# Gathered value rows of the last 64 tokens: the first rows land in the running sums, a fourth place lies over the residual, and a round's two sums stand in two tiles

## What is computed

```python
def peer(h, wq, sub_keys, u_tab, v_tab):
    ...
        qq = (hx @ wq).reshape(pb, PEER_HEADS, 2, PEER_HALF)
        s = jnp.einsum('nhcd,hckd->nhck', qq, sub_keys).astype(jnp.float32)
        s1, i1 = lax.top_k(s[:, :, 0], PEER_TOPK)
        s2, i2 = lax.top_k(s[:, :, 1], PEER_TOPK)
        ...
        top, sel = lax.top_k(cand, PEER_TOPK)
        eidx = jnp.take_along_axis(cidx, sel, axis=-1)
        g = jax.nn.softmax(top, axis=-1)
        a = jax.nn.gelu(jnp.einsum('nd,nhkd->nhk', hx, u_tab[eidx]).astype(jnp.float32), approximate=False)
        w = (g * a).astype(hx.dtype)
        return jnp.einsum('nhk,nhkd->nd', w, v_tab[eidx])
    ...
    x = x + (ga * y_conv + gb * y_nsa) @ P['w_o']
    x = x + peer(rmsnorm(x, P['norm_ffn']), P['peer_wq'], P['peer_sub_keys'], P['peer_u'], P['peer_v'])
```

## Time and profile before

| | |
|---|---|
| median of three runs | 1196.44 us (1188.22 to 1201.93) |
| the profiled execution: its time | 1196.77 us |
| its span, first to last instruction | 1195.1 us |
| PE busy | 96% of the span |
| DVE busy | 75% |
| POOL busy | 52% |
| ACT busy | 51% |
| HBM read, written | 246.18 MB, 20.09 MB |
| v stage, first tile's start to the span's end | 829.37 to 1195.1 us |

### The profile page before, as it was taken

The page is one execution under the profiler, slowest core; times in us unless marked ns, Lnnn a source line. Parts: engine busy times, 40 slices in busy tenths (PEclk is TensorE's granted clock), DMA queues, the critical chain, the costliest instruction groups (busy, mean ns, idle before and its releaser), DMA issues.

```text
span 1195.1 us, 22982 instructions
## 1 busy us (share of the span) xinstructions
PE 1147.2 (96%) x8076; PEld 1087.6 (91%) x8076; DVE 897.1 (75%) x1599; ACT 604.5 (51%) x1159; POOL 624.2 (52%) x515
## 2 busy tenths in 40 slices
PE   7999999999999999999999999999979999988998
PEld 6698989978899999999999999999878998877998
DVE  6478456654686799999957887886776887876985
ACT  5355455432353454554556777755434554443552
POOL 2422234431000287877688777031787888887820
PEclk9999899899999999999999999999999999999999
DMA  6773439767765267677675666688888998888973
GB/s 245 271 228 88 142 104 344 231 191 258 211 235 174 98 180 174 167 171 187 171 184 144 162 168 162 195 262 287 313 297 270 318 321 287 290 290 283 326 274 124
DMA packets 129251, 263.64 MB, mean 221 GB/s; under 512 B 34608, under 2 KB 68976, under 8 KB 128432
## 3 DMA queue, kind: packets, MB, share of 16 engines
q1 hardware_dynamic: 89568, 208.08, 52.6%
q0 software_dynamic: 36848, 50.69, 17.2%
q10 hardware_dynamic: 2720, 3.40, 0.8%
HBM read 246.18 MB, written 20.09 MB: 223 GB/s over the span
## 4 chain that ended last, share of the span: by engine, by line
PE 73%; POOL 9%; issue 7%; DVE 5%; DMA 3%; ACT 2%; POOLq 1%; another core or an unknown queue 0%; ACTq 0%; DVEq 0%
PE ps L2297 26%; PE ps L2302 13%; PE ps L2372 9%; PE ps L2379 5%; POOL arena L677 5%; POOL arena L686 2%; PE ps L1843 2%; PE ps L2007 2%; PE ps L2110 2%; PE ps L1863 2%; DMA arena<-in_v,aux 2%; POOL aux L677 1%; PE ps L2148 1%; PE ps L2346 1%; PE ps L2115 1%
## 5 line engine op out<-in xcount | busy, mean ns | idle before, releaser
L1046 ACT ACTIVATE w_hi<-ring 128x1024 fp32r<-128x1024 f32 x280 | 296.8, 1060 | 366.3 <-issue 171.8
L1543 DVE TENSOR_TENSOR w_lo<-ring,w_hi 128x1024 fp32r<-128x1024 f32 x271 | 330.0, 1222 | 117.3 <-ACT w_hi L1046 83.2
L2297 PE MATMUL ps<-h_hi,w_hi 128*128 128x288 f32 x1088 | 294.9, 299 | 0.5 <-ACT w_hi L1046 0.5
L666 POOL DMA_INDIRECT gates<-arena x128 | 241.6, 1887 | 68.8 <-issue 44.9
L2297 PE MATMUL ps<-h_lo,w_hi 128*128 128x288 f32 x1024 | 277.3, 295 | 0.0
L2297 PEld LDWEIGHTS ps<-h_hi,w_hi 128*128 128x128 f32 x1088 | 205.5, 189 | 1.2 <-ACT w_hi L1046 1.0
L677 POOL DMA_INDIRECT arena<-in_v,aux x110 | 149.2, 1357 | 88.4 <-PE ps L2346 49.1
L2297 PEld LDWEIGHTS ps<-h_lo,w_hi 128*128 128x128 f32 x1024 | 192.8, 188 | 0.0
L2302 PE MATMUL ps<-h_hi,w_lo 128*128 128x288 f32 x1088 | 168.1, 297 | 2.1 <-DVE w_lo L1543 2.1
L2372 PE MATMUL ps<-h_hi,w_hi 128*128 128x448 f32 x672 | 154.5, 373 | 4.9 <-issue 3.0
L2302 PEld LDWEIGHTS ps<-h_hi,w_lo 128*128 128x128 f32 x1088 | 152.3, 189 | 2.6 <-DVE w_lo L1543 2.6
(11 more groups left out here) (377 smaller groups left out, 1968.1 us busy)
## 6 DMA issues: line engine op xcount, KB each, us to landing
ring<-in_uT SPq DMA_DIRECT2D x128, 512.0 KB
ring<-in_v SPq DMA_DIRECT2D x128, 512.0 KB
ring<-in_wout SPq DMA_DIRECT2D x32, 512.0 KB
ring<-in_wT SPq DMA_DIRECT2D x28, 512.0 KB
gates<-aux SPq DMA_DIRECT2D x32, 256.0 KB, 5.9
ring<-in_wtok SPq DMA_DIRECT2D x8, 512.0 KB
act_kept<-arena SPq DMA_DIRECT2D x32, 128.0 KB
aux<-gates SPq DMA_DIRECT2D x16, 256.0 KB
```

What stands on the lines that cost most here:

```text
L666: pool.indirect_dma_start(gates, bass.IndirectOffsetOnAxis(rt("gi")[:, P + s:P + s + 1].bitcast(U32), 0), rt("gi")[:, s:s + 1], None, comp ...
L1046: act.activation(w_hi[e % 2][:, :], ring[:, (W_O + e) % RING, :], ACT.Copy).then_inc(S["w_high"], 1)
L1543: dve.tensor_tensor(w_lo[e % 2][:, :], ring[:, (W_O + e) % RING, :], w_hi[e % 2][:, :].bitcast(F32), ALU.subtract)\
L2297: last = pe.matmul(ps[:, bank, 0:NT], w_hi[e % 2][:, k * P:(k + 1) * P], mov[:, k, :], start=(k == 0 and mov is mov_hi), stop=False, skip_ ...
```

## The change

1. **Places.** Slot 0's rows go straight into the two running sums (`IN_SUMS`), and DVE multiplies them there in place. Slots 1 and 2 take places 0 and 1. A fourth place, `OVER_X`, is the first 2048 columns of `xT`; slots 3, 6, 10, 14 and so on to 26 lie there. The place over the gates serves slots 7, 11, ... From slot 27 on, three places are left.
2. **POOL's order.** Twelve row transfers instead of eight are issued before the wait for the activations (slots 1, 2, then slot 0, whose x = 0 part also waits for `qq_or_sums`, the last use of that memory in the u stage). The wait for PE's tile (`row_tile(i)`) is gone; what remains is `rows_used` of the slot before in the place, once `lo_used` for the end of the u stage, once `weighed`, and `s_weights` before the values.
3. **Tiles of the sums.** x = 0 stands in a slot's tile and x = 1 in the next. Slots 0 to 3 are at tiles 8, 11, 14, 17; slots 4 to 26 at 20 to 104, one every 27/7 = 3.857 tiles; slots 27 to 31 at 107, 110, 113, 116 and 119 (x = 1 at 120).
4. **The residual.** Since `xT` is a place until slot 26, SP reads it back at tile 115 (`X1_AT`) and not at tile 8. The constant stays at tile 8.

```diff
+OVER_X, OVER_GATES, IN_SUMS = HELD, HELD + 1, HELD + 2
+LAST_OVER_X = 26
+def slot_place(i):
+    if i == 0:
+        return IN_SUMS
+    if i < FOUR:
+        return i - 1
+    return i % FOUR if i <= LAST_OVER_X else (OVER_GATES, 0, 1)[(i - LAST_OVER_X - 1) % 3]
 def slot_tile(i):
-    return row_tile(i + 1) + 2 if i < WIDER - HELD else row_tile(i + 2) + 1
-def slot_place(i):
-    return i % HELD if i < WIDER else (i - WIDER + HELD) % (HELD + 1)
+    if i < FOUR:
+        return 8 + 3 * i
+    return 20 + (i - FOUR) * 27 // 7 if i <= LAST_OVER_X else slot_tile(LAST_OVER_X) + 3 * (i - LAST_OVER_X)
...
-SLOT_AT = {slot_tile(i): i for i in range(SLOTS)}
-SUM_AT = PK - 6
+SLOT_AT = {slot_tile(i) + x: (i, x) for i in range(SLOTS) for x in range(2)}
+SUM_AT, X1_AT = PK - 6, PK - 13
...
                 if t == 2 * RING:
                     sp.wait_ge(S["lo_used"], E_V)
+                    sp.dma_start(e_ident, A["consts"][:, CONST["ident"][0]:CONST["ident"][1]]).then_inc(S["x1_back"], 16)
+                if t == X1_AT:
+                    sp.wait_ge(S["rows_used"], 2 * LAST_OVER_X + 2)
                     sp.dma_start(xT[:, :, :], x1_kept).then_inc(S["x1_back"], 16)
-                    sp.dma_start(e_ident, A["consts"][:, CONST["ident"][0]:CONST["ident"][1]]).then_inc(S["x1_back"], 16)
...
-            for i in range(HELD):
+            for i in (1, 2):
                 for x in range(2):
                     gather_rows(x, i)
+            gather_rows(1, 0)
+            pool.wait_ge(S["qq_or_sums"], Q_TILES + GROUPS)
+            gather_rows(0, 0)
             for i in range(2):
                 pool.wait_ge(S[f"act_out{i}"], 16 * PK // STAGE // 2)
             for k in range(4 * FOUR):
                 gather_value(k)
-            for i in range(HELD, SLOTS):
-                pool.wait_ge(S["lo_used"], E_V + row_tile(i))
-                if i == WIDER:
+            pool.wait_ge(S["lo_used"], E_V)
+            for i in range(3, SLOTS):
+                if i == FOUR + OVER_GATES:
                     pool.wait_ge(S["weighed"], PIECES_IN)
                 for x in range(2):
                     if earlier_slot(i) >= 0:
                         pool.wait_ge(S["rows_used"], 2 * earlier_slot(i) + x + 1)
                     gather_rows(x, i)
...
-            def weigh_slot(i):
+            def weigh_slot(i, x):
-                if i % FOUR == 0:
+                if i % FOUR == 0 and x == 0:
...
-                for x in range(2):
-                    w = e_weights[:, NS * x + i:NS * x + i + 1]
+                w = e_weights[:, NS * x + i:NS * x + i + 1]
...
                 if t in (SUM_AT + 1, SUM_AT + 3):
                     dh = (t - SUM_AT) // 2
                     dve.wait_ge(S["so_turned"], 2 + dh + 1)
+                    dve.wait_ge(S["x1_back"], 32)
...
                 if t == HALF:
-                    dve.wait_ge(S["x1_back"], 32)
+                    dve.wait_ge(S["x1_back"], 16)
```

More of the change, by code:

```diff
@@ L703, in _ @@
                     gather_rows(x, i)
-                if i % FOUR == HELD:
-                    pool.wait_ge(S["s_weights"], 2 + i // FOUR + 1)
-                for k in range(2 * (i + 2 * FOUR - HELD), 2 * (i + 2 * FOUR - HELD) + 2):
+                for k in range(4 * FOUR + 2 * (i - 3), 4 * FOUR + 2 * (i - 3) + 2):
                     if k < 2 * SLOTS:
+                        b = k // (2 * FOUR)
+                        if k % (2 * FOUR) == 0:
+                            pool.wait_ge(S["s_weights"], 2 + b - 2 + 1)
                         gather_value(k)
@@ L1806, in weigh_slot @@
                 dve.wait_ge(S["s_weights"], 2 + i // FOUR + 1)
[L1807 to L1815 removed]
+                w = e_weights[:, NS * x + i:NS * x + i + 1]
+                dve.wait_ge(S[row_sems[x][slot_place(i)]], row_base[x][slot_place(i)] + 32 * place_uses(i))
+                if i == 0:
+                    last = dve.tensor_scalar(e_sums[x], e_rows[x][IN_SUMS], w, None, ALU.mult)
+                else:
+                    dve.wait_ge(S["rows_used"], 2 * (i - 1) + x + 1)
+                    last = dve.scalar_tensor_tensor(out=e_sums[x], in0=e_rows[x][slot_place(i)], scalar=w, in1=e_sums[x], op0=ALU.mult, op1=ALU.add)
+                last.then_inc(S["rows_used"], 1)
             mov_low_part(1)
```

23 lines of the change are left out of this document (7 added, 16 removed).

## The result

| | before | after |
|---|---|---|
| median | 1196.87 us (1184.06 to 1210.69, 20 runs) | 1188.13 us (1178.22 to 1205.67, 20 runs) |
| profiled execution, span | 1195.1 us | 1181.0 us (its time 1182.7) |
| tile 0 to tile 122 of the v stage | 829.37 to 1171.77 | 828.14 to 1157.72 |

The ratio is 0.994, 95% interval 0.991 to 0.997: 7 us faster by the ratio, 9 by the medians, where 26 us were forecast. The time lies outside the range (1161 to 1186).

What follows compares the result with a forecast made beforehand. POOL's issuing of transfers was taken to bound the v stage, losing 36 us. Tile 122's end at 1146.2 plus a 20.8 us tail gave 1167.0, the residual's 2 us 1169 of span, forecast as 1171 us, range 1161 to 1186.

Steps and rivals of the forecast that it cites:

- What bounds the kernel: v stage: 36 us of PE time are lost, because POOL's issuing of transfers makes rows late, not the number of places.
- Part 1: POOL in the v stage: starts slot 3 at 855.8 us, issues 164 transfers, values' slots at 1.67 us each, ends at 1136.3.
- Part 2: Rows against DVE's sums: next to nothing lost up to slot 26; in the last five slots POOL is slower than wanted.
- Part 3: End of the v stage: last rows land at 1140.3, tile 122 ends at 1146.2, plus 20.8 us gives a span of 1167.0.
- the floor: The span with no loss in the v stage: 123 tiles of 2.51 us and the unchanged tail, 1158.9 us.
- rival 2: v stage: ring loads become the bound and ACT's three long idles (10.7 us) add to the sum; 1182 us, chance 0.13.
- Rival 1: v stage: POOL keeps up with DVE's less dense work and nearly nothing is lost; 1161 us, chance 0.14.
- Rival 4: v stage: DVE is late for another reason, such as its own 86% load; within 12 us of before, chance 0.06.
- Rival 3: v stage: without a pace POOL's issues grow to 2.0 us each, deciding from 1.88; 1216 us, chance 0.07.
- The pace is gone: POOL's start in the v stage: no 2.54 us hold by PE's tile, so slot 3 starts at 855.8 us.
- Part 4: Remaining edits: moving the residual's read costs 2 us (0 to 4.3); two tiles for sums and the fourth place count nothing.
- The rule against the trace: DVE and POOL exclude each other at SBUF, so POOL would run faster beside less dense DVE work, making the sum too high.

Runs made afterwards that it cites:

- b_noval: The kernel before the change without the 48 value gathers that follow the first 16; 1164.94 us, ratio 0.970.
- a_tiny: The changed kernel with row gathers of slots 1 to 31 bringing 16 of 512 columns, as many transfers; 1193.56 us, ratio 0.988.
- a_halfring: The changed kernel with SP loading only half of every v tile, columns 0 to 511 of 1024; 1188.39 us, ratio 0.990.
- a_paced: The changed kernel with a pace put back: POOL waits before a slot's rows until PE is within nine tiles of the slot's tile; 1178.74 us, ratio 0.985.
- a_paced_2: a_paced run again on another chip; 1175.37 us, ratio 0.984.
- a_one: The changed kernel with both sums of a slot put back into one tile; 1192.08 us, ratio 0.991.
- a_nogates: The changed kernel without the 17 gate loads that SP puts between the loads of v tiles 0 to 16; 1183.86 us, ratio 0.987.
- third chip: Ran the changed kernel with POOL zero writes replacing 48 value gathers (1161.94 us), with three waits a slot (1163.86), and with whole-row gathers plus pace (1160.98).

## Why the prediction was wrong

**What bounds the kernel: right.** 36 us were lost, and the number of POOL's transfers made the rows late: b_noval has no row wait and 0.970 of the time. But rows were not all of it: about 13 of the 36 us stood in tiles that waited for a late signal of PE (8 and 9, 25 to 27, 93 to 95; an estimate from the tiles' lengths less 2.51 us).

**Part 1, POOL's work: right to a microsecond.** Timeline of POOL after: the first row gather of slot 3, and the last two of slot 31.

```profile
856.18 0.95 POOL L684 DMA_INDIRECT xT<-in_v,aux  x1 [0.30 <-issue]
...
1133.26 1.83 POOL L684 DMA_INDIRECT arena<-in_v,aux  x1 [0.30 <-issue]
1135.39 0.95 POOL L684 DMA_INDIRECT arena<-in_v,aux  x1 [0.30 <-issue]
```

Forecast were a start at 855.8, `xT` as the target and an end at 1136.3; it was 1135.39 + 0.95 = 1136.34. But it contains 20 us of waits for places, so POOL was faster than 1.67 us a transfer, (280.2 - 20.4) / 164 = 1.58. Two errors met, so the match is luck.

**Part 2, rows in time: right.** 0.2 us of idle before the sums.

**Part 3, the sum: this step failed.** It took "tile 122 ends when the last rows have been added" and let the floor cover all that isn't rows. Tile 122 started at 1157.72, not at 1143.7, and not because of any row: the last sums stood early and PE was late all the same, which the prediction had named as the sign of a wrong mechanism. The term that failed is the loss beside rows: 0 beyond the residual's 2 us in the sum, 23 us in the trace, where `w_hi` and `w_lo` wait for signals that PE gives up to 7.6 us late. The 8 us that the sum left for rows were not lost, so two errors partly cancel. It could be seen before: ACT's idles of 4.30, 3.62 and 2.81 us with an unseen releaser, which the prediction read as late ring loads and priced in rival 2 at 10.7 us and a chance of 0.13. Each of the three ends 0.07 us after an update of `hi_used` (852.32, 911.67, 1100.26), for halves that PE had ended 3.6 to 5.7 us earlier.

**Rival 2, ring loads, was nearest in time (1182) and wrong in cause.** Its own test, ACT's waits for the ring over 15 us, came out at 5.0. a_tiny and a_halfring take the bytes away, and the time stays.

**The other rivals.** Rival 1 asked for under 1.6 us a transfer; POOL had 1.58, and the time was still lost elsewhere. Rival 4 (the losses stay, for another reason) holds the measured time within its 12 us, at a chance of 0.06, but it named DVE's own load. In mechanism it is the nearest, since it alone has DVE late for a reason other than rows or loads. Rival 3's rate of 1.88 us was never near.

**"The pace is gone" was priced as a gain; it was a loss.** a_paced and a_paced_2 stand at 0.985 and 0.984, the changed kernel at 0.994, so dropping the pace costs 10 to 12 us. The rest of the change is worth 18 to 19 us, where 26 were forecast. The prediction took the pace for a mere delay (5.9 us in 6 waits). With it, signals are late less often (27 and 26 starts for 43).

**Part 4.** *Residual's read*: forecast 2 us, measured none; from 1130.19 us, when SP issues it, to tile 122 every tile takes 2.51 or 2.52 us. Moving it away from tile 8 didn't win the 2.6 us carried over from there either: that cluster was no work of the residual's, and grew from 3 to 10 us. *Two tiles for the sums*: nothing, as forecast (a_one). *Fourth place*: "a place isn't what POOL waits for" is wrong for the changed kernel, where POOL waits 20 us for places; what those waits are worth isn't shown, since a fourth place was not tried alone. *Gate loads*: at most a few us (a_nogates).

**The rule against the trace.** The Trainium skill, "SBUF — State Buffer", section "SBUF: two separate sides", has DVE and GpSimd take turns at a shared port. For POOL the trace agrees in direction: its issue takes 0.95 us where DVE rests and often 1.4 to 2.0 beside it. It is tempting to read the late `w_lo` as the other half of the rule, POOL holding DVE up. The trace doesn't bear that out: each of them starts 0.09 us after PE's signal. The same section says that ACT's port waits on no one, and ACT's idles of 3 to 15 us are no evidence against it, since ACT too was waiting for PE's signals.

**What stays open.** Why PE's updates come late beside POOL's indirect issues is not known; that they do, and that they come within 2.2 to 2.4 us of a burst's end, is. Nor is it known why a cluster begins where it does, or why the third chip's executions have none.

## What to carry to other kernels

Count the indirect transfers that GpSimd issues, not their bytes: here 48 tiny ones less, or two merged into one, gave 2.0 to 3.0% of the time (23 to 36 us by the ratios), and thirty times fewer row bytes gave next to nothing. When an engine on the path idles with a releaser that the profile doesn't see, list what the code has it wait for, and see when each of these had ended, before calling it a late load or a held-up engine. A wait that paces such an engine may be useful work; price its removal from both sides.
